# A transformer stack and a delta-rule layer on one core: three stores of the output, a halved output unit, an earlier copy of the query, other places for modulation products

## What is computed

```
mod = silu(c) @ ada_w[i] + ada_b[i]          # six pieces: sh1 sc1 g1 sh2 sc2 g2
h = rms_norm(x, gain) * (1 + sc1) + sh1
x = x + g1 * mixer(h)                        # 0: stick-breaking, 1: MoBA, 2: sliding window, 3: stick-breaking
h = rms_norm(x, gain) * (1 + sc2) + sh2
x = x + g2 * (silu(h @ w_gate) * (h @ w_up)) @ w_down     # 2816 hidden columns
```

## Time and profile before

| | us |
|---|---|
| median of 3 runs (lowest, highest) | 2159.41 (2149.91, 2163.64) |
| own time of the profiled execution | 2151.61 |
| its span, first to last instruction | 2149.8 |

### The profile page before, as it was taken

The page is one execution under the profiler, slowest core; times in us unless marked ns, Lnnn a source line. Parts: engine busy times, 40 slices in busy tenths (PEclk is TensorE's granted clock), DMA queues, the critical chain, the costliest instruction groups (busy, mean ns, idle before and its releaser), DMA issues.

```text
span 2149.8 us, 33122 instructions
## 1 busy us (share of the span) xinstructions
PE 1937.1 (90%) x13890; PEld 1509.8 (70%) x13890; DVE 1341.1 (62%) x1412; ACT 917.4 (43%) x1367; POOL 110.1 (5%) x139
## 2 busy tenths in 40 slices
PE   4888999999899998999999899989998888688998
PEld 3666887655687754777777677778787777666877
DVE  6775775563687744697755588875447645446564
ACT  3445444233544334544355544445335211335443
POOL 1001000110000000000000100002000220000000
PEclk9998999999999999999999999999989999989999
DMA  8753886553697742698843367973222000224552
GB/s 324 274 216 118 273 285 241 203 193 137 209 324 279 275 166 69 208 355 286 296 133 122 99 225 256 335 266 129 68 79 78 3 4 4 95 89 151 176 177 98
DMA packets 215113, 393.37 MB, mean 183 GB/s; under 512 B 11305, under 2 KB 130101, under 8 KB 199605
## 3 DMA queue, kind: packets, MB, share of 16 engines
q1 hardware_dynamic: 214453, 391.12, 52.3%
q0 software_dynamic: 512, 0.13, 0.0%
HBM read 390.17 MB, written 1.05 MB: 182 GB/s over the span
## 4 chain that ended last, share of the span: by engine, by line
PE 59%; DVE 22%; ACT 10%; issue 6%; DMA 2%; DVEq 0%; POOL 0%; SPq 0%; ACTq 0%; POOLq 0%
PE G L2134 12%; PE G L2136 12%; PE G L2135 12%; DVE w_lo L1430 10%; ACT w_hi L935 5%; PE G L2340 5%; DVE acc L1483 5%; PE G L2416 2%; PE A L2710 2%; ACT full L1000 1%; PE A L2722 1%; DVE act_st L1768 1%; PE G L2724 1%; PE A L2253 1%; PE A L2182 1%
## 5 line engine op out<-in xcount | busy, mean ns | idle before, releaser
L1430 DVE TENSOR_TENSOR w_lo<-raw,w_hi 128x2048 fp32r<-128x2048 f32 (+2 forms) x237 | 513.4, 2166 | 316.1 <-ACT w_hi L935 305.3
L935 ACT CAST w_hi<-raw 128x2048 fp32r<-128x2048 f32 (+1 forms) x230 | 427.6, 1859 | 554.0 <-PE G L2136 500.9
L2134 PE MATMUL G<-w_hi,h_hi 128*128 128x512 f32 (+2 forms) x1232 | 492.2, 400 | 27.9 <-issue 11.3
L2135 PE MATMUL G<-w_lo,h_hi 128*128 128x512 f32 (+2 forms) x1232 | 482.4, 392 | 0.0
L2136 PE MATMUL G<-w_hi,h_lo 128*128 128x512 f32 (+2 forms) x1232 | 482.3, 391 | 0.0
L1483 DVE SCALAR_TENSOR_TENSOR acc<-raw,c_col,acc 128x2048 f32<-128x2048 f32 x120 | 282.0, 2350 | 60.5 <-DMA raw<-in_ada_w 39.2
L2134 PEld LDWEIGHTS G<-w_hi,h_hi 128*128 128x128 f32 x1232 | 236.2, 192 | 83.4 <-issue 38.6
L2134 PE MATMUL G<-w_hi,act_hi 128*128 128x512 f32 (+2 forms) x640 | 254.5, 398 | 34.2 <-DVE w_lo L1430 22.3
L2136 PEld LDWEIGHTS G<-w_hi,h_lo 128*128 128x128 f32 x1232 | 235.7, 191 | 49.4
L2135 PEld LDWEIGHTS G<-w_lo,h_hi 128*128 128x128 f32 x1232 | 236.3, 192 | 44.9
L2135 PE MATMUL G<-w_lo,act_hi 128*128 128x512 f32 (+2 forms) x640 | 249.9, 391 | 0.0
(11 more groups left out here) (396 smaller groups left out, 2090.9 us busy)
## 6 DMA issues: line engine op xcount, KB each, us to landing
raw<-in_ada_w SPq DMA_DIRECT2D x96, 1024.0 KB, 5.4
raw<-in_ffn_w_gate SPq DMA_DIRECT2D x88, 512.0 KB, 3.9
raw<-in_ffn_w_up SPq DMA_DIRECT2D x88, 512.0 KB, 5.1
raw<-in_ffn_w_down SPq DMA_DIRECT2D x40, 1024.0 KB, 5.6
raw<-in_w_mlp SPq DMA_DIRECT2D x32, 1024.0 KB, 5.3
raw<-in_w_ada SPq DMA_DIRECT2D x24, 1024.0 KB, 5.4
raw<-in_w_in SPq DMA_DIRECT2D x18, 1024.0 KB, 5.0
raw<-in_sb_w_in SPq DMA_DIRECT2D x32, 512.0 KB, 4.9
```

The costliest lines, as they stand in the source:

```text
L935: nc.scalar.copy(w_hi[:, c % 2, 0:len(kts), 0:n], raw[:, slot].rearrange("p (k n) -> p k n", k=UNIT_K)[:, 0:len(kts), 0:n])\
L1430: return nc.vector.tensor_tensor(w_lo[:, c % 2, ks, 0:n], raw[:, slot].rearrange("p (k n) -> p k n", k=UNIT_K)[:, ks, 0:n], w_hi[:, c % 2, ...
L2134: nc.tensor.matmul(banks[t][:, 0:n], x_hi[:, kt, ts], w_hi[:, u % 2, i, 0:n], start=st, stop=False)
L2135: nc.tensor.matmul(banks[t][:, 0:n], x_hi[:, kt, ts], w_lo[:, u % 2, i, 0:n], start=False, stop=False)
```

## The change

1. The output leaves in three stores instead of one: the first 512 columns, then the second 512 of token tile 0, then of tile 1. The last panel's residual is done by `last_residual`, one tile at a time.
2. In the stick-breaking mixers (layers 0 and 3) step V of group 3 moves from slot 13 to 14. The output unit of rows 512 to 1023 for the first panel is cut in two `half_unit`s of 12 matmuls; the first stands between C and V of group 3, the second behind V and the r2 sums. The r1 sums move from behind the second output unit to ahead of the first one.
3. Layer 0's products: the third of slot 0 and its followers come one slot later each, so that slot 0 has two instead of three and slot 5 two instead of one.
4. The four products in mixer 2 (slots 0, 1, 3, 5) move into layer 1's feed-forward, which then has 24. With 24 products, layers 1 and 2 spread them evenly over positions 2 to 29; before, layer 1 had 20 and layer 2 had 24, at positions 2 to 30 without 20 to 23. Positions in layer 1 now: 2 to 6, 8 to 12, 14 to 18, 20 to 24, 26 to 29 (before: 2 to 5, 7 to 9, 11 to 13, 15 to 18, 24 to 26, 28 to 30); layer 2 now the same (before: 2 to 13, 15 to 19, 24 to 30).
5. In the context norm ScalarE copies the query panel (`lat_evac(0, 0)`) between the second and third split, ahead of its cast, instead of behind the fourth split.

```
-                    13: [("C", 3), ("V", 3)]}
+                    13: [("C", 3)], 14: [("V", 3)]}
...
-                   {n: [(2, ADA_U - 4 + i)] for i, n in enumerate((0, 1, 3, 5))}, {}]
+        ADA_MIX = [{}, {n: [(1, 2 * KT + i)] for i, n in enumerate((0, 1, 3, 5, 7, 9, 11, 13))}, {}, {}]
...
-            ADA_MIX[0].setdefault(max(0, i - 2), []).append((0, KT + i))
+            ADA_MIX[0].setdefault((0, 0, 1, 2, 3, 4, 5, 5, 6, 7, 8, 9, 10, 11, 12, 13)[i], []).append((0, KT + i))
...
-                slot = 2 + (i + min(i, twice)) * 29 // (ADA_U + twice) if twice else FF_FREE[i * len(FF_FREE) // count]
+                slot = 2 + (i + min(i, twice)) * 29 // (ADA_U + twice) if count == ADA_U else FF_FREE[i * len(FF_FREE) // count]
...
+            sp.wait_ge(x_ready, 4 * DEPTH + 5)
+            sp.dma_start(out_t[:, :, 0:512], x_res[:, :, 0:512]).then_inc(out_done, 16)
+            sp.wait_ge(x_half, 2 * DEPTH + 2)
+            sp.dma_start(out_t[:, 0, 512:D], x_res[:, 0, 512:D]).then_inc(out_done, 16)
             sp.wait_ge(x_ready, 4 * DEPTH + 6)
-            sp.dma_start(out.rearrange("b (t p) d -> p (b t) d", p=P), x_res).then_inc(out_done, 16)
+            sp.dma_start(out_t[:, 1, 512:D], x_res[:, 1, 512:D]).then_inc(out_done, 16)
...
-                        if n in (nq + 1, nq + 2):
-                            modulation(l, ("r1", "r2")[n - nq - 1])
+                        if n in (nq - 1, nq + 2):
+                            modulation(l, "r1" if n < nq else "r2")
...
+            def query_out():
+                lat_evac(0, 0)
+                convert()
...
+            norm(LAT, 32, 16, act_hi, x=ctx_raw, piece="cc", ahead=convert, between=query_out)
...
-                residual(um + 16 * part + 16, 1, 1, LAT)
+                if part == 0:
+                    residual(um + 16, 1, 1, LAT)
+            for t in range(NT):
+                last_residual(t, um + 32, 1, LAT)
```

TensorE's part of the stick-breaking mixer, after the last projection unit (nq = 12; po are the two output panels; `unit` takes weights, activations and banks as before):

```
+                modulation(l, "r1")
                 po = [k.panel("dve"), k.panel("dve")]
+                pe.wait_ge(split_lo, f_o[1] - k.native)
+                for j in range(2):
+                    wait_panel_free(po[j])
+                    unit(act_hi, act_lo, range(4), G[...po[j]...], True, False)
+                    if j == 0:
+                        pe.wait_ge(mod_out, k.sums)
+                    steps(nq + j)
+                def half_unit(g):       # waits hi_ready, lo_ready; for both tiles, kt = 2g and 2g + 1: hi hi, hi lo, lo hi
...
+                pe.wait_ge(split_lo, f_o[2] - k.native)
+                half_unit(2)
+                steps(nq + 2)
+                modulation(l, "r2")
+                pe.wait_ge(split_lo, f_o[3] - k.native)
+                half_unit(3).then_inc(gemm_done, 1)
+                k.u += 1
+                unit(act_hi, act_lo, range(4, 8), G[...po[1]...], False, True, tiles=True)
```

More of the change, by code:

```diff
@@ L1210, in _ @@
             norm(LAT, 0, 0, x_end=4 * LAT, piece="c0", between=convert)
[L1211 to L1214, removed]
             def square(x, n, dst):
@@ L1307, in _ @@
             for n in range(LAT_UNITS):
-                if n and n % 2 == 0:
+                if n > 2 and n % 2 == 0:
                     lat_evac(n // 2 - 1, 1 if LAT_PANELS[n // 2 - 1][3] else 0)
@@ L2366, in sb_mixer @@
                     steps(n)
+                modulation(l, "r1")
                 po = [k.panel("dve"), k.panel("dve")]
[L2368 to L2373, removed]
-                        unit(act_hi, act_lo, range(4 * h, 4 * h + 4), G[2 * (po[j] % 2):2 * (po[j] % 2) + 2], h == 0, h == 1, tiles=h == 1 and j == 1)
-                        steps(n)
-                        if n == 2 * len(panels) + 1:
-                            modulation(l, "r1")
-                        if n == 2 * len(panels) + 2:
-                            modulation(l, "r2")
-                        n += 1
+                nq = 2 * len(panels)
@@ new lines, in sb_mixer @@
+                pe.wait_ge(split_lo, f_o[1] - k.native)
+                for j in range(2):
+                    wait_panel_free(po[j])
+                    unit(act_hi, act_lo, range(4), G[2 * (po[j] % 2):2 * (po[j] % 2) + 2], True, False)
+                    if j == 0:
+                        pe.wait_ge(mod_out, k.sums)
+                    steps(nq + j)
+                def half_unit(g):
+                    u = nth_converted[k.u]
+                    pe.wait_ge(hi_ready, u + 1)
+                    pe.wait_ge(lo_ready, u + 1)
+                    for t in range(NT):
+                        bank, ts = G[2 * (po[0] % 2) + t], slice(t * P, t * P + P)
+                        for i in range(2):
+                            kt, part = 2 * g + i, 2 * (g - 2) + i
+                            nc.tensor.matmul(bank, act_hi[:, kt, ts], w_hi[:, u % 2, part], start=False, stop=False)
+                            nc.tensor.matmul(bank, act_hi[:, kt, ts], w_lo[:, u % 2, part], start=False, stop=False)
+                            ins = nc.tensor.matmul(bank, act_lo[:, kt, ts], w_hi[:, u % 2, part], start=False, stop=g == 3 and i == 1)
+                    return ins
@@ L2382, in softmax_mixer @@
+                pe.wait_ge(split_lo, f_o[2] - k.native)
[5 more added lines that the diff above has]
+                k.u += 1
+                unit(act_hi, act_lo, range(4, 8), G[2 * (po[1] % 2):2 * (po[1] % 2) + 2], False, True, tiles=True)
             def softmax_mixer(l, kind):
@@ L2871, in _ @@
                         pe.wait_ge(split_lo, f_a - 8 + 2 * (h + 1) - k.native)
-                        unit(act_hi, act_lo, range(4 * h, 4 * h + 4), G[2 * (pn % 2):2 * (pn % 2) + 2], h == 0, h == 3)
+                        unit(act_hi, act_lo, range(4 * h, 4 * h + 4), G[2 * (pn % 2):2 * (pn % 2) + 2], h == 0, h == 3, tiles=part == 1 and j == 1 and h == 3)
                         if j == 0 and h == 0:
```

9 lines of the change are left out of this document (6 added, 3 removed).

## The result

The changed kernel takes 2140.8 us in the median of 6 runs (2134.92 to 2146.95), the kernel before 2158.91 us beside them (6 runs, 2149.91 to 2163.64). The ratio is 0.992, 95% interval 0.9902 to 0.9938: -18.1 us, where -16.8 was forecast. A second comparison on another chip gave 2137.05 against 2156.7 us, ratio 0.9906 (0.9884 to 0.9927).

What follows compares the result with a forecast made beforehand. TensorE was taken to set the end and, where it stands still, a VectorE or ScalarE step. The terms (-2.9 - 4.0 - 1.0 - 2.5 - 0.8 - 2.2 - 3.4) sum to -16.8 us: 2159.4 to 2142.6 us, range 2129 to 2153.

Steps and rivals of the forecast that it cites:

- Term 1: Layer 0, slot 0: one product fewer lets unit 2 start 2.57 us earlier at full clock; -2.9 us in sum.
- The clock part: Layer 0, matmuls behind the idle before unit 2: with only 1.6 us idle they run at 2.4 GHz, saving 1.5 us.
- Term 2: Layers 0 and 3: half a unit fills the wait before V3, r1 sums move early; -4.0 and -1.0 us.
- the split as next late: Layers 0 and 3: V3's split releases the second half unit some 4.9 us after V3's start.
- Term 3: Layer 2's attention: without its four products, waits for loads and before the key-value transposes shrink; -2.5 us.
- Term 4: Feed-forward of layers 1 and 2: products spread evenly; +0.3 us in layer 1, -1.1 in layer 2, together -0.8.
- Rival A: Feed-forward positions 20 to 23 stall TensorE while it waits for low parts; 2147.1 us, chance 0.17.
- B: Feed-forward of layers 1 and 2: VectorE is over-full, each moved product adds 2.57 us; 2164.0 us, chance 0.04.
- Term 5: Context norm: the earlier query copy ends some 4 us sooner, but only about 2.2 us come through; -2.2 us.
- The wait that would take over: Last block: unit 4 then waits about 2.7 us for its low part from VectorE.
- Rival C: Shortened idles before unit 2 and at the query copy don't pay: slow clock, late load, longer next wait; 2147.7 us, chance 0.14.
- Term 6: Tail: less arithmetic and a quarter of the bytes stand behind the last matmul; -3.4 us, -3.0 by the skill's fit.

Runs made afterwards that it cites:

- Run 8: Changed kernel with layer 0's products as before, three of them in slot 0 again; ratio 0.9937 to the kernel before.
- run 1: Kernel before with only the new tail (three stores, last residual tile by tile); ratio 0.9999 to the kernel before.
- run 6: Changed kernel with the output projection of layers 0 and 3 as before (no halved unit, r1 sums late); ratio 0.994 to the kernel before.
- runs 9 and 10: Four products back in the third attention: on the changed kernel, ratio 0.9904; with GpSimd's later clearing and VectorE's earlier low part as well, 0.9899.
- run 11: Changed kernel with the 24 products of layers 1 and 2 at positions leaving out 20 to 23; ratio 0.9909 to the kernel before.
- run 3: Changed kernel with VectorE taking unit 4's low part earlier, ahead of its wait for GpSimd's rotation of the query; ratio 0.9902 to the kernel before.
- changed_again: The changed kernel itself measured again, on another chip; 2137.05 us against 2156.7 us for the kernel before, ratio 0.9906.
- run 7: Changed kernel with the output unit whole and V of group 3 in slot 13, r1 sums still early; ratio 0.9966 to the kernel before.
- run 12: The same run as changed_again: the changed kernel unaltered, beside the kernel before; ratio 0.9906.
- run 2: Changed kernel with the query panel copied behind the fourth split again; ratio 0.9928 to the kernel before.
- run 4: Changed kernel with two of GpSimd's three clearing memsets delayed until after the second norm's first split; ratio 0.9884 to the kernel before.

## Why the prediction was right, and where it was not
The time was right, in part by luck; the steps are right in part.

**Term 1, one product fewer ahead of unit 2 (-2.9).** Right in kind: unit 2 started 2.7 us earlier, at full pace. Run 8 gives -3.1 less slow time (152.6 - 155.7) where the forecast without its clock part is -1.4: none of the product was paid back. The clock part (-1.5) is no fixed price: run 1's trace, which has the code of before here, idled 3.42 us at this place and ran on at a granted 1.00, while run 8's ran at half pace for longer than the earlier trace rows.

**Term 2, halved unit and r1 (-4.0 and -1.0).** Inside the projection the mechanism is confirmed, to 0.3 us at the second half's start; V3 to the end of the last unit takes 13.3 and 12.9 us, forecast 13.06. For the two mixers run 6 gives -3.1 and -1.4 less slow time, -4.2 and -3.1 traced. The failed step is what came behind. The text named the split as next late, and did not ask what the earlier c12 sums start: they release GpSimd's memsets, which then fall on the norm's second scaling. Against the 1.21 us of before that scaling is 1.3 to 1.5 us longer in layer 3 and, in 5 of the 7 traces with this projection and the early clearing, 1.7 to 2.0 us longer in layer 0. With what else grew in feed-forward 3 it cancels the waits saved (run 6); the term came out as pace, which it had not counted.

**Term 3, attention without products (-2.5).** Mixer 2 is 3.3 us shorter less slow time (109.2 to 105.9), but runs 9 and 10 give the four products only 1.6 to 2.0 of it, and as traced nothing that can be told. The 3.6 us between the first two profiles were in part a slow stretch: with the same code the second trace of before took 111.4 instead of 114.6. The other 1.5 us can be placed, but not explained. TensorE idles 13.4 and 13.2 us in this stage with the code of before, 11.7 and 12.0 in runs 9 and 10, and 10.5 in the changed kernel. With the products back the product in slot 3 waits 2.48 and 2.86 us for its load and not 4.59, though that load is issued at the same point of the stage as before (21.0 and 21.1 us into it), so the key-value transposes wait 0.40 and 0.69 us and not 1.53. Why the load lands earlier is open.

**Term 4, feed-forward placement (-0.8).** Layer 1 +0.5 less slow time (forecast +0.3). Layer 2: two lengths for the same code, 202.4 and 204.1 less slow time, around the 203.2 of before; the -1.1 cannot be seen. The low-part waits there were 0.79 and 2.26 us in the first trace, none and 1.57 in the second, where 0 and 1.21 were forecast: that step failed in its size. Rival A fell with run 11, and B with it, as the feed-forward parts of layers 1 and 2 together grew by 0.6 us less slow time, not by 20.

**Term 5, context norm (-2.2).** Wrong: 0. The wait that would take over was named and nearly sized (2.7, measured 3.28), and unit 4 did start 2.2 us earlier in its stage. The step that failed is that a new idle time was priced at its own length alone. Some of the matmuls behind it ran at half pace: 1486.44 to 1507.87 took 21.4 us, 1489.26 to 1508.47 in the kernel before 19.2. That is 2.2 us, the whole gain. In the windows (columns as in the earlier trace rows), first of the kernel before, then of the changed one, the granted clock there is 1.00 and 0.89:

```profile
1489.26:1508.47 19.21, 18.38 (x90) 15.26 (x90) 10.88 (x20) 7.14 (x12) 3.04 (x9) 1.00 0.30 101
```
```profile
1486.44:1507.87 21.43, 20.60 (x89) 16.87 (x89) 12.23 (x26) 8.58 (x16) 3.03 (x9) 0.89 0.32 102
```

Over the whole stage TensorE idles 6.05 us before and 5.26 after, only 0.8 less, and one slow stretch is exchanged for another: half-pace matmuls for 3.5 us behind the idle of 5.22, for 4.8 us behind that of 3.28. The idle is not the whole cause: in run 3, which has none there, 3.42 us (1474.18 to 1477.60) still ran at a granted 0.50, shortly behind the 32 one-column matmuls that also stand ahead of the 3.28 us. Rival C had this right for this term and wrong for term 1. After the 2.51 us of layer 3 the first matmul was slow too. The section of the Trainium skill that the prediction names (TensorE: Matmul & The Clock Gate, HAM oscillation) warns of longer gaps only; here the traces decide against taking comfort from that.

**Term 6, the tail (-3.4).** Right: -3.1, alone and together. The fit of the Trainium skill that the prediction uses (DMA: Bandwidth & Descriptors, Anatomy of one DMA) is given there for the path from GpSimd, and these stores go by SyncE's queue; from issue to the end of the span the whole store took 4.4 us and the last quarter 2.4, where it gives an estimated 4.4 and 2.6; the -3.0 worked out from it came nearer than the -3.4.

**Where the rest came from.** Less slow time (span x mean granted clock, averaged over the runs of changed_again's comparison) the kernel before takes 2070.1 us (17 runs) and the changed one 2060.9 (5 runs): -9.2, give or take some 3.5 since single runs scatter by 3.4, while the forecast without its 1.5 us of clock was -15.3. (This measure also shortens idle time at a low clock, which the one for stages does not.) The other 10.5 us are clock: its mean rose from 0.9608 to 0.9654. In the first comparison the six changed runs give 2062.1 us and 0.9638. So two errors met, an overcounted 6 us of waits and an uncounted 9 us of pace, and the total is right by luck to that extent. For the halved unit the lift of the clock is shown: the mean clock is 0.9614 in the 12 executions of run 7 and 0.9613 in the 6 of run 6, against 0.9654 in run 12 and 0.9647 in run 11, which have it and stood beside them. For the product in slot 0 it is likely (0.9628 in the 6 executions of run 8 against 0.9654), for the others not shown. In feed-forward 3 the changed kernel is 3.3 to 4.6 us longer less slow time; of the 4.2 us of idle that TensorE gains there in the first trace, 2.4 stand ahead of the norm's transposes and 1.0 ahead of one low part (2.53 us before, 3.56 now); the cause of the latter stays open.

## What to carry to other kernels
When a step comes earlier, look at every engine that it releases, also those off the critical path, and at what runs beside their next instruction: a clearing on GpSimd that had just missed VectorE's scaling now meets it, and a wait on GpSimd that makes it later was worth 0.44% against run 2 on the same chip, a kernel as fast as the changed one. The kernel before had such collisions already, in layers 1 to 3, so that wait removes more than the change had added. Look behind TensorE's idle times as well as at them: in the 13 traces other than run 4's, 63 of 113 idle times of 2 to 3 us that began at full clock, and 52 of 53 of 3 to 6 us, had a mean granted clock under 0.75 over the first us behind them, at the half level 0.2 us more for each matmul. An idle time that is only exchanged for another may bring nothing. Before crediting an edit with a stage's gain, trace that stage once more with the same code.

## What the runs showed of the hardware
A TENSOR_SCALAR of 128x1024 fp32 from SBUF to SBUF on VectorE (0.75 us) does not run beside a GpSimd MEMSET of 128x2048 (1.8 us): it ends 0.55 us behind it and takes 1.04 to 2.80 us. VectorE's TENSOR_TENSOR beside the same memsets kept its 1.22 us (1024 columns). Beside a GpSimd instruction that reads, it is otherwise: one multiplication of the rotation (128x128, two inputs) took 2.50 us instead of 0.45 beside VectorE's low part (run 3). The Trainium skill (SBUF — State Buffer, Who interferes with whom) states both: the two engines share a pair of ports as an exclusive lock; `tensor_scalar` can use it and then contends with GpSimd, while an instruction with two SBUF inputs contends only with a GpSimd instruction that reads SBUF; whoever is first blocks the other. The traces agree, with one addition: a scaling recorded as starting up to 0.42 us before the memset can lose as well.
